# The last norm's root on ScalarE and VectorE, and one supertile's stores and loads on SyncE's queue

## What is computed

```python
h = rmsnorm(x, norm1_g); z = h @ w_in                  # [pool a | u | v], 3 x 512
x = x + concat(pool_mixer(a), u * (W_s v + b)) @ w_out # gelu on u and v
f = rmsnorm(x, norm2_g) @ w_up                         # 1024 -> 4096
x = x + square(relu(f)) @ w_down                       # 4096 -> 1024
y = rmsnorm(x, normf_g)                                # x / sqrt(mean(x*x) + eps) * g
```

## Time and profile before

| what | value |
|---|---|
| runs, median of 3 | 1253.15 us |
| profiled execution, span of its slowest core (core 3); the page gives no other time of it | 1253.2 us |
| spans of the eight cores | 1246.4 to 1253.2 us |
| TensorE busy on core 3 | 1232.4 us, 98% |
| VectorE, ScalarE, GpSimd busy | 501.0, 372.4, 100.8 us |
| DMA traffic | 240.48 MB, mean 192 GB/s |

### The profile page before, as it was taken

The page is one execution under the profiler, slowest core; times in us unless marked ns, Lnnn a source line. Parts: engine busy times, 40 slices in busy tenths (PEclk is TensorE's granted clock), DMA queues, the critical chain, the costliest instruction groups (busy, mean ns, idle before and its releaser), DMA issues.

```text
span 1253.2 us, 19036 instructions; the slowest of 8 cores (1246.4 to 1253.2 us)
## 1 busy us (share of the span) xinstructions
PE 1232.4 (98%) x6777; PEld 652.2 (52%) x6777; DVE 501.0 (40%) x921; ACT 372.4 (30%) x717; POOL 100.8 (8%) x182
## 2 busy tenths in 40 slices
PE   8999999999999999999999999999999999999996
PEld 3455545545545554554555455455545545554554
DVE  5764434444533442543344254334425433541312
ACT  5353312134322330432233043223304322320411
POOL 6010000001010000100000010000001000000000
PEclk9999999999999999999999999999999999999999
DMA  8999978549448537745853774685387458547751
GB/s 176 175 225 215 229 172 186 146 127 320 143 134 256 205 131 224 234 168 156 271 193 133 221 237 168 159 267 195 132 223 236 168 161 264 144 146 228 254 203 51
DMA packets 90671, 240.48 MB, mean 192 GB/s; under 512 B 57665, under 2 KB 57729, under 8 KB 67794
## 3 DMA queue, kind: packets, MB, share of 16 engines
q1 hardware_dynamic: 77616, 186.59, 47.1%
q0 software_dynamic: 12784, 52.34, 18.5%
q10 hardware_dynamic: 178, 0.33, 0.1%
HBM read 214.40 MB, written 34.43 MB: 199 GB/s over the span
## 4 chain that ended last, share of the span: by engine, by line
PE 94%; DMA 3%; POOL 1%; issue 1%; DVE 0%; ACT 0%; POOLq 0%; SPq 0%; DVEq 0%; ACTq 0%
PE ps L703 30%; PE ps L761 28%; PE ps L587 9%; PE ps L430 7%; PE ps L665 7%; PE ps L685 6%; PE ps L455 4%; DMA WOUT<-w_out 2%; PE ps L783 2%; DMA X<-xall 1%; PE ps L535 1%; PE ps L350 1%; POOL RS L328 0%; POOL RS L322 0%; ACT JUNK L315 0%
## 5 line engine op out<-in xcount | busy, mean ns | idle before, releaser
L703 PE MATMUL ps<-H2T,RING 128*128 128x384 bf16 x2304 | 385.3, 327 | 0.5 <-DVE X L689 0.5
L761 PE MATMUL ps<-RING,ST 128*128 128x512 bf16 x1632 | 353.7, 379 | 0.0
L703 PEld LDWEIGHTS ps<-H2T,RING 128*128 128x128 bf16 x2304 | 224.3, 98 | 148.3 <-issue 1.9
L761 PEld LDWEIGHTS ps<-RING,ST 128*128 128x128 bf16 x1632 | 159.7, 98 | 191.7
L315 ACT ACTIVATE JUNK<-X 128x1024 bf16<-128x1024 f32 (+2 forms) x104 | 106.4, 1023 | 438.9 <-DVE X L768 290.1
L707 ACT ACTIVATE ST<-ps 128x384 bf16<-128x384 f32 x288 | 140.5, 490 | 208.7 <-PE ps L703 208.7
L709 DVE TENSOR_TENSOR ST<-ST 128x384 bf16<-128x384 bf16 x288 | 95.9, 355 | 185.9 <-ACT ST L707 185.6
L768 DVE TENSOR_TENSOR X<-ps,X 128x512 f32<-128x512 f32 x48 | 33.2, 691 | 219.8 <-PE ps L761 219.8
L430 PE MATMUL ps<-HT,WAU 128*128 128x384 bf16 (+1 forms) x640 | 106.8, 326 | 2.2 <-DMA WAU<-w_au 2.2
L430 PEld LDWEIGHTS ps<-HT,WAU 128*128 128x128 bf16 x640 | 62.2, 98 | 44.4 <-issue 3.6
L685 PE MATMUL ps<-RING,ST 128*128 128x512 bf16 x384 | 83.7, 379 | 0.2 <-issue 0.2
(11 more groups left out here) (99 smaller groups left out, 728.3 us busy)
## 6 DMA issues: line engine op xcount, KB each, us to landing
RING<-scr SPq DMA_DIRECT2D x144, 1024.0 KB, 5.6
RING<-w_mlp POOLq DMA_DIRECT2D x16, 1024.0 KB, 19.9
scr<-RING SPq DMA_DIRECT2D x16, 1024.0 KB, 10.6
yall<-X POOLq DMA_DIRECT2D x30, 512.0 KB, 11.3
X<-xall POOLq DMA_DIRECT2D x27, 512.0 KB, 5.5
X<-xall SPq DMA_DIRECT2D x6, 512.0 KB, 6.9
WOUT<-w_out POOLq DMA_DIRECT2D x2, 1024.0 KB, 26.5
WAU<-w_au POOLq DMA_DIRECT2D x3, 512.0 KB, 7.2
```

What stands on the lines that cost most here:

```text
L703: i_ = e.matmul(bank(ub)[:, 0:TOK], lhsT=RING[s][:, k, (m % 4) * 128:(m % 4 + 1) * 128], rhs=H2T[:, k, :], start=(k == 0), stop=(k == 7))
L761: i_ = e.matmul(bank(n)[:, :], lhsT=ST[:, kg * 8 + kk, n * 128:(n + 1) * 128], rhs=RING[s][:, kk, :], start=(kg == 0 and kk == 0), stop=(k ...
```

## The change

The last supertile's root is no longer an add and a power on GpSimd, but a square root on ScalarE (the sum of earlier parts and eps as its bias) into a new buffer RT and a reciprocal on VectorE. A dummy square root of RT stands behind the last ReLU; RT is set to 1 at the start. In the middle, supertile 0's y stores and supertile 3's x loads are issued by SyncE, and the calls are in another order.

```diff
@@ setup
+        RT = sb("RT", [128, 4], F32)
+        add("pool", lambda e: e.memset(RT[:], 1.0), writes=[("RT", n) for n in range(4)])
@@ gen_L: the queue becomes an argument
-        def gen_L(i):
+        def gen_L(i, q="pool"):
-                add("pool", lambda e, b=b, n=n, t=t: e.dma_start(out=X[b][:, n, :], in_=xall[t * 128:(t + 1) * 128, :]),
-                    writes=[("X", b, n)], dma=f"xld{b}_{n}")
+                add(q, lambda e, b=b, n=n, t=t: e.dma_start(out=X[b][:, n, :], in_=xall[t * 128:(t + 1) * 128, :]),
+                    writes=[("X", b, n)], dma=f"xld{b}_{n}{q}")
@@ gen_tail
-            add("pool", lambda e: e.tensor_tensor(out=RS["f"][:, n:n + 1], in0=S, in1=SSE[:, n:n + 1], op=ALU.add),
-                reads=[("SSc", "2", col), ("SSE", n)], writes=[("RS", "f", n)])
-            norm_pow("f", n, n + 1)
+            add("act", lambda e: e.activation(out=RT[:, n:n + 1], in_=S, func=AF.Sqrt, bias=SSE[:, n:n + 1], scale=1.0),
+                reads=[("SSc", "2", col), ("SSE", n)], writes=[("RT", n)])
+            add("dve", lambda e: e.reciprocal(out=RS["f"][:, n:n + 1], in_=RT[:, n:n + 1]),
+                reads=[("RT", n)], writes=[("RS", "f", n)])
@@ gen_final: the stores become a function of their own
-                fin_y[(b, n)] = add("pool", lambda e, n=n, t=t: e.dma_start(out=yall[t * 128:(t + 1) * 128, :], in_=X[b][:, n, :]),
-                                    reads=[("X", b, n)], dma=f"yst{b}_{n}")
+            if store:
+                gen_ystore(i, tiles)
+
+        def gen_ystore(i, tiles, q="pool"):
+            b = i % NXB
+            for n in tiles:
+                t = i * NT + n
+                fin_y[(q, b, n)] = add(q, lambda e, n=n, t=t: e.dma_start(out=yall[t * 128:(t + 1) * 128, :], in_=X[b][:, n, :]),
+                                    reads=[("X", b, n)], dma=f"yst{b}_{n}{q}")
@@ the middle
-        for h in range(2):
-            gen_pair_DN(3, 0, h)
-            gen_pair_DN(3, 1, h)
-            gen_final(h)
-            if h == 0:
-                gen_L(3)
+        gen_pair_DN(3, 0, 0)
+        gen_pair_DN(3, 1, 0)
+        gen_final(0, store=False)
+        gen_pair_DN(3, 0, 1)
         ring_next(0, 11)
+        gen_ystore(0, range(NT), "sp")
+        gen_pair_DN(3, 1, 1)
         ring_next(0, 15)
+        gen_final(1)
+        gen_L(3, "sp")
@@ behind gen_UP(i, 30, 32)
+                if last:
+                    add("act", lambda e: e.activation(out=JUNK[:, 0:4], in_=RT[:], func=AF.Sqrt),
+                        reads=[("RT", n) for n in range(4)], writes=["JUNK"])
```

More of the change, by code:

```diff
@@ L749, in gen_tail_out @@
             for hi, q in enumerate(("act", "sp")):
-                fin_y[(n, hi)] = add(q, lambda e, hi=hi: e.dma_start(
+                fin_y[("end", n, hi)] = add(q, lambda e, hi=hi: e.dma_start(
                     out=yall[t * 128:(t + 1) * 128, hi * 512:hi * 512 + 512], in_=XG[:, n, hi * 512:hi * 512 + 512]),
@@ L790, in gen_DN_last, with gen_final @@
                 gen_tail_out(i, n)
-        def gen_final(i, tiles=None, squares_done=False):
+        def gen_final(i, tiles=None, squares_done=False, store=True):
             b = i % NXB
```

## The result

The changed kernel takes 1247.99 us (median of 4 runs, 1246.79 to 1248.74); the kernel before, run beside it, 1254.11 (4 runs, 1252.9 to 1256.64). A second series of the same two gave 0.9937 (0.9915 to 0.9959). The profiled execution took 1248.57 us, its span is 1247.0. In all ratios here, executions in which one half of the chip ran at a visibly lower clock are left out.

The account below looks back on a forecast made before the run. TensorE works 98% of the span and core 3 sets the time, 1253.2 us; less 3.85 in the middle, core 1 sets the end at 1249.6; less 0.6 for the last norm gives 1249.0 us, range 1247.6 to 1252.8.

Parts of the forecast that it names:

- The middle: Supertile 2's up projection: core 3 loses 3.85 us less, so core 1 sets the end at 1249.6 instead of 1253.2.
- Core 3's excess wait and the clock behind it: TensorE's wait for HB, 2.18 us beyond core 1's 0.64, and 1.68 us of lower clock after it, both go.
- The x tiles in time: Supertile 3's third x load on SyncE's queue lands at 292.7 to 297.7, wanted at 302.0: at least 4.3 us early.
- No stall for q5: The ring load of q5 behind the x loads lands at 296.0 to 301.0, wanted at 303.5: no TensorE stall.
- The slower rival: q5's ring load stalls TensorE in the up projection, slower than before from a landing of 306.0 on; chance 0.07.
- The last norm: At the end, the root on ScalarE and VectorE moves the last store's issue 0.60 us earlier.
- The base: The sum starts from core 3's span, 1253.2 us, taken as level with the runs' median of 1253.15.
- The late x tiles: Rival: GpSimd's stores are served first, x stays late, only the tail is gained: 1252.6; chance 0.13.
- the table per tile: Rival: Square is not in the root's table, so ScalarE loads 1.28 us on the last tile's path: 1250.3; chance 0.05.
- Another stretch sets the end: Rival: a core that starts late in most runs sets the end, 1250 to 1252; chance 0.11.

Follow-up runs that it names:

- the queues alone: The changed kernel without the dummy root and with the last norm's add and power back on GpSimd; ratio 0.9983 to the kernel before, 2.1 us less.
- The last norm alone: The kernel before with only the last root moved to ScalarE and VectorE, stores and loads staying on GpSimd's queue; ratio 0.9967 to the kernel before.
- last run of "Order or queue": The changed kernel with supertile 3's x loads back on GpSimd's queue, only supertile 0's stores on SyncE's; ratio 0.9973 to the kernel before.

## Why the prediction was right and where it was wrong

*The middle: right in its mechanism, too large in its size.* Core 3's excess wait and the clock behind it went, on every core, and 0.64 us stayed. The size, 3.6 us from 1253.2 to 1249.6, was that of one execution; over many the queues alone give 2.1 us (0.4 to 3.8), of which 0.5 is the shorter DRAIN. That the slowest core isn't always one with the late tile is the likely reason; it was not tested.

*The x tiles in time: right, by a sum that was simpler than what ran.* In the two profiled executions of the changed kernel the third tile landed 14.2 to 22.7 us behind the up projection's start, against the 15.8 to 20.8 that the bytes gave (292.7 and 297.7 less 276.89), and was wanted at 25.1: in time, but outside the bounds at both ends. The sum took all queues as one line at 314 GB/s. That came near because x stood in SyncE's order; in the two runs that left it on GpSimd's queue the same bytes landed 20.6 to 30.4 and, behind supertile 1's stores, 35.7 to 38.1 us behind.

*No stall for q5: not quite.* It landed 18.8 to 26.8 us behind the up projection's start; the bounds were 19.1 to 24.1, so the upper one was 2.7 us too low. Two cores of 16 waited for it, 0.34 and 0.92 us, in the place of HB's 0.64, so that one lost 0.28 us. The slower rival (a landing at 306, with a loss of clock) didn't come.

*The last norm: the step that failed.* The forecast was "the last issue moves by 0.60", bounds from 0.2 lost to 0.9 gained. The issue did move, by 0.64, with a root of 0.29 and a reciprocal of 0.16 where 0.28 and 0.15 were taken. But the sum ended at the last issue and took what follows as fixed, without a reason. It wasn't: GpSimd's DRAIN, 7.19 us behind its last instruction, and not the store, closed the barrier. The term is 4.1 us (9.69 less 5.56): 3.3 between SyncE's DRAIN and GpSimd's, 0.8 from the earlier landing. With 4.1 in place of 0.6 the sum would have been 1249.6 - 4.1 = 1245.5 by spans, and core 1 came to 1245.1. The forecast of 4.2 us lies nearer to the 6.5 measured than its terms do to theirs, and that is luck in part: the middle was some 2 us too high, the tail 3.5 too low.

*The base: a span read as a time.* The sum started from 1253.2, a span, as level with the median time, 1253.15. In every execution on record, of either kernel, the time is 1.5 to 1.6 us above the longest span; 1253.2 belongs to a time of 1254.7 or so. As a span the forecast of 1249.0 missed the changed kernel's 1247.0 by 2.0 us; beside the time of 1247.99 the miss looks half as large as it was.

*Rivals.* The late x tiles and the table per tile fell by the trace. Without the dummy there is one load, of 1.28 us, the root follows 0.01 us behind it, and no other load comes before the end: one set serves Square, root and Copy. The Trainium skill, page "ScalarE: Activation LUTs", section "What ACT_TABLE_LOAD costs", gives 2.66 us for a switch, 1.28 of it the load; the load agrees, the rest was not seen here. "Another stretch sets the end" is partly true: the changed kernel's slowest core, 4, lost its time in the start. Its up projection starts at 278.71, that of the fastest, core 5, at 273.80, and their spans differ by as much, 4.9 us. Of this 2.51 us are a wait for WV at 44.94; its clock in the first 60 us is 0.97, core 5's 1.00.

## What to carry to other kernels

Sum a tail to the last instruction of the program, not to the last store: look which engine's DRAIN closes the barrier, and let the engine with the long one finish early, by giving its last work to engines that are through sooner. When a transfer is late, ask on which queue it stands and what stands ahead of it there, before asking when it was issued; and look whether the clock falls behind a wait before pricing it: behind 2.82 us in the kernel before and 2.76 in "The last norm alone" it did, behind 3.13 us on core 7 of the last run of "Order or queue" it stayed at 1.00. Compare spans with spans and times with times.

## What the runs showed that was not expected

Behind late arithmetic, GpSimd's DRAIN at the end of the program lasts about 0.082 us for every DMA that GpSimd issued in the whole program, though the last of them had landed over 60 us earlier; a single late add of 0.2 us on that engine put the end 3.0 us further behind the last matmul. On one core GpSimd's queue and SyncE's moved equal numbers of packets in 24 us, 665 and 663, but 2.46 MB in rows of 4 KB beside 4.88 in rows of 8 KB. With supertile 1's stores ahead of the three loads on GpSimd's queue, the kernel was 13 us slower than with the stores of supertile 0 and the loads on SyncE's.
